# First expert pair: token rows gathered straight into turned form, shorter norm and mask steps, another order of the last output quarters

## The reference, cut to what matters

```python
x = x + jnp.einsum('bte,ed->btd', merged, w_out)
h2 = rmsnorm(x, ffn_norm_w)                       # mean of squares, + EPS, rsqrt, times the weight
x = x + moe_ffn(h2, w_router, b_router, w_up, b_up, w_down, b_down)

def moe_ffn(h, ...):                              # 264 tokens, 32 experts, D = 1024
    logits = h @ w_router + b_router
    top_vals, top_idx = lax.top_k(logits, 4)      # ties go to the lower expert
    gates = softmax(top_vals)
    ...                                           # for each expert e, on the rows of its tokens:
    u = xb @ w_up[e] + b_up[e]                    # 1024 -> 2048
    a = glu * sigmoid(1.702 * glu) * (lin + 1)    # glu, lin: even and odd columns, clamped at 7
    y = a @ w_down[e] + b_down[e]                 # 1024 -> 1024, times the gate, added to its token
```

## Time and profile before

| | |
|---|---|
| median of three runs | 1151.85 us |
| the profiled execution's own time | 1151.45 us |
| its span (first to last instruction) | 1149.5 us |
| busy: TensorE, VectorE, ScalarE | 95%, 39%, 16% |
| TensorE's granted clock | 0.993 of full speed |
| moved by the transfers | 444.34 MB, 387 GB/s over the span |
| share of the chain that ended last | TensorE 61%, DMA 36% |

### The profile page before, as it was taken

How to read it: one execution, slowest core, us unless ns; L and a number is a source line. 1 busy time by engine, 2 the same in 40 slices (tenths; PEclk the granted TensorE clock), 3 DMA queues, 4 the chain that set the end, 5 groups by cost and what they waited for, 6 DMA issues and landing times.

```text
span 1149.5 us, 14796 instructions
## 1 busy us (share of the span) xinstructions
PE 1095.8 (95%) x5914; PEld 495.3 (43%) x5943; DVE 444.3 (39%) x878; ACT 184.8 (16%) x394; POOL 88.5 (8%) x161
## 2 busy tenths in 40 slices
PE   9999999999999999999999999999999999999997
PEld 6688898553333333333333333333333333333332
DVE  4867786753343233232323232323232323232322
ACT  2133231220321111010101010101010101010101
POOL 1775115000000000000000000000000000000000
PEclk9999999999999999999999999999999999999999
DMA  9945639989999999999999999999999999999996
GB/s 318 328 135 158 196 92 341 399 328 429 422 418 427 424 429 433 432 429 433 433 429 433 433 429 433 434 428 434 433 428 434 433 428 434 433 428 434 425 423 267
DMA packets 52628, 444.34 MB, mean 387 GB/s; under 512 B 13037, under 2 KB 19309, under 8 KB 35677
## 3 DMA queue, kind: packets, MB, share of 16 engines
q1 hardware_dynamic: 46136, 435.83, 91.0%
q0 software_dynamic: 5600, 7.32, 2.4%
q10 hardware_dynamic: 852, 0.64, 0.2%
HBM read 439.78 MB, written 2.37 MB: 385 GB/s over the span
## 4 chain that ended last, share of the span: by engine, by line
PE 61%; DMA 36%; DVE 1%; ACT 1%; issue 1%; SPq 0%; ACTq 0%
PE pA L1964 30%; PE pB L1964 23%; DMA ring<-in_w_up 21%; DMA ring<-in_w_down 10%; PE pM L1964 6%; DMA area<-in_w_up 5%; PE pM L1967 1%; PE pA L1967 1%; ACT area L1199 0%; DVE x L1816 0%; DVE hn L1858 0%; DVE area L1860 0%; DVE area L1852 0%; ACT area L1176 0%; ACT area L1028 0%
## 5 line engine op out<-in xcount | busy, mean ns | idle before, releaser
L1964 PE MATMUL pA<-ring,hn 128*64 128x512 f32 x1536 | 354.2, 604 | 23.0 <-DMA ring<-in_w_up 23.0
L1964 PEld LDWEIGHTS pA<-ring,hn 128*64 128x64 f32 x1536 | 105.4, 138 | 220.3 <-issue 187.4
L1964 PE MATMUL pB<-ring,area 128*64 128x512 f32 (+2 forms) x784 | 171.5, 591 | 6.6 <-DMA ring<-in_w_down 5.7
L1964 PE MATMUL pB<-area,ring 128*128 128x132 f32 (+2 forms) x928 | 140.3, 342 | 0.5 <-ACT area L1028 0.5
L1964 PE MATMUL pA<-area,hn 128*64 128x512 f32 x512 | 119.3, 610 | 9.9 <-DMA area<-in_w_up 9.8
L1964 PEld LDWEIGHTS pB<-area,ring 128*128 128x128 f32 (+1 forms) x928 | 115.7, 175 | 22.4 <-issue 3.2
L1964 PEld LDWEIGHTS pB<-ring,area 128*64 128x64 f32 (+2 forms) x784 | 58.5, 136 | 101.1 <-issue 87.8
L1816 DVE TENSOR_TENSOR x<-pM,x 128x512 f32<-128x512 f32 x60 | 40.1, 691 | 148.2 <-PE pM L1964 148.1
L1187 ACT ACTIVATE area<-area 128x512 f32<-128x512 f32 x30 | 18.9, 631 | 386.3 <-DVE area L1799 386.3
L1731 DVE COPY conv_row<-pM 128x512 f32<-128x512 f32 x30 | 20.6, 686 | 146.2 <-PE pM L1964 146.2
L1964 PE MATMUL pB<-area 128*64 128x512 f32 (+2 forms) x300 | 67.2, 550 | 1.2 <-DVE area L1264 1.2
(11 more groups left out here) (335 smaller groups left out, 936.6 us busy)
## 6 DMA issues: line engine op xcount, KB each, us to landing
ring<-in_w_up SPq DMA_DIRECT2D x36, 4096.0 KB, 29.8
ring<-in_w_down SPq DMA_DIRECT2D x18, 4096.0 KB, 29.2
area<-in_w_up SPq DMA_DIRECT2D x12, 4096.0 KB, 30.2
ring<-in_w_up SPq DMA_DIRECT2D x17, 2048.0 KB, 15.2
area<-in_w_down SPq DMA_DIRECT2D x6, 4096.0 KB, 30.0
ring<-in_w_in SPq DMA_DIRECT2D x22, 1024.0 KB, 12.1
ring<-in_w_up SPq DMA_DIRECT2D x14, 1024.0 KB, 8.9
ring<-in_w_down SPq DMA_DIRECT2D x13, 1024.0 KB, 25.9
```

The source lines that it names most:

```text
L1964: return pe.matmul(out, w, m, start=start, stop=stop, skip_group_check=True)
```

## The change

Four things are changed.

1. The gather of the first pair works the other way round: eight groups of 128 columns of `hn` (every fourth column of a half, so that the order is that of the weights' rows) are stationary, `pick` moves, and the product stands in PSUM in turned form at once. The copies to `xrow` and the eight transposes are gone; VectorE multiplies each pair of groups from PSUM into `xsT`. Groups 0 to 3 stand before `up(0)`, the three products of each of groups 4 to 7 stand between `up(1)` and `up(2)`.
2. `rms`: the scale by 1/D and the addition of EPS are done by ScalarE's root.
3. The mask: the count of larger logits is the start of the running sum, in place of an operation of its own.
4. `BRANCH`: both pieces of the last half product stand together, `x_cols` 4 and 5 behind them, `ahead` is gone, and the first transpose of `x_cols` 4 releases the place of chunk 5.

```diff
-          ("logits", 0), ("part", (0, 6, KT)), ("half", 0), ("part", (1, 0, 4)), ("count", 0), ("part", (1, 4, 6)),
-          ("x_cols", 4), ("part", (1, 6, KT)), ("half", 1), ("ahead", 1), ("x_cols", 5), ("rms", 1), ("logits", 1),
-          ("gather", 1), ("count", 1), ("gather", 2)]
+          ("logits", 0), ("part", (0, 6, KT)), ("half", 0), ("part", (1, 0, 4)), ("count", 0), ("part", (1, 4, KT)),
+          ("half", 1), ("x_cols", 4), ("x_cols", 5), ("rms", 1), ("logits", 1),
+          ("gather", 1), ("count", 1)]
...
-            return pB[:, n, 0:256] if n < 2 else pA[:, 512 * n:512 * n + 256]
+            if n == 0:
+                return pB[:, :, 0:128]
+            if n == 1:
+                return pA[:, 1024:2048].rearrange("p (k c) -> p k c", k=2)[:, :, 0:128]
+            return pA[:, 512 * n:512 * n + 256].rearrange("p (k c) -> p k c", k=2)
...
-                    nc.scalar.activation(stat[0:r, 8 + a:9 + a], stat[0:r, 8 + a:9 + a], ACT.Sqrt).then_inc(norm_rt, 1)
+                    s1 = stat[:, 5:6] if a == 1 else stat[0:r, 2 * a + 1:2 * a + 2]
+                    nc.scalar.activation(stat[0:r, 8 + a:9 + a], s1, ACT.Sqrt, bias=stat[0:r, 62:63],
+                                         scale=1.0 / D).then_inc(norm_rt, 1)
...
-            for n in (1, 3):
-                act.wait_ge(first_full, n + 1)
-                f = slice(256 * n, 256 * n + 256)
-                nc.scalar.activation(xrow[:, f], first_xs(n), ACT.Copy).then_inc(first_rows_act, 1)
...
-                    V.tensor_scalar(stat[0:r, 8 + a:9 + a], s1, 1.0 / D, EPS, ALU.mult, ALU.add).then_inc(norm_in, 1)
...
-                    V.tensor_scalar(stat[rows_, 56 + a:57 + a], stat[rows_, 56 + a:57 + a], -1.0, float(TOPK),
-                                    ALU.mult, ALU.add)
-                    link(V.tensor_tensor_scan(rank[rows_, :], cst[rows_, C_ONE:C_ONE + NE], e, 0.0,
+                    link(V.tensor_tensor_scan(rank[rows_, :], cst[rows_, C_ONE:C_ONE + NE], e, stat[rows_, 56 + a:57 + a],
...
-            for n in (0, 2):
+            for n in range(4):
                 dve.wait_ge(first_full, n + 1)
-                f = slice(256 * n, 256 * n + 256)
-                V.tensor_copy(xrow[:, f], first_xs(n)).then_inc(first_rows, 1)
                 if n == 0:
                     dve.wait_ge(fnorm_loaded, 16)
-                for k in (n, n + 1):
-                    V.tensor_tensor(xsT[:, 2 * k:2 * k + 2, :], misc_bank()[:, 0:256].rearrange("p (k s) -> p k s", k=2),
-                                    fw[:, 2 * k:2 * k + 2, :], ALU.mult).then_inc(misc_free, 1)
+                V.tensor_tensor(xsT[:, 2 * n:2 * n + 2, :], first_xs(n),
+                                fw[:, 2 * n:2 * n + 2, :], ALU.mult).then_inc(first_rows, 1)
...
-            def first_gather(n):
-                return matmul(first_out(n), pick[:, 0].rearrange("p e s -> p (e s)"), piece(hn[:, 0, :], n), stop=False)
+            def turned(t, k):
+
+                h = 512 * (k // ROWS)
+                return t[:, h + k % ROWS:h + 512:ROWS]
+
+            def first_gather(k):
+
+                matmul(first_xs(k // 2)[:, k % 2], turned(hn[:, 0, :], k), pick[:, 0].rearrange("p e s -> p (e s)"), stop=False)
+
+            def first_samples(k):
+
+                matmul(first_xs(k // 2)[:, k % 2], turned(s_parts[0:96], k), s_pick[0:96].rearrange("p e s -> p (e s)"),
+                       start=False, stop=False)
+
+            def first_rest(k):
+
+                mm = matmul(first_xs(k // 2)[:, k % 2], turned(hn[:, 1, :], k), pick[:, 1].rearrange("p e s -> p (e s)"),
+                            start=False)
+                if k % 2:
+                    mm.then_inc(first_full, 1)
...
-                    if a == 2:
+                    if a in (2, 4):
                         mm.then_inc(ring_free, 1)
...
-                    for k in range(2 if a == 1 else 0, KT):
+                    for k in range(KT):
...
-            for n in range(4):
-                matmul(first_out(n), pick[:, 1].rearrange("p e s -> p (e s)"), piece(hn[:, 1, :], n),
-                       start=False).then_inc(first_full, 1)
-                if n:
-                    if n < 3:
-                        first_turn(n - 1)
+            for k in range(ROWS):
+                first_rest(k)
...
                     if first and e == 0:
-                        if c == 1:
-                            first_turn(2)
-                            first_turn(3)
-                        pe.wait_ge(misc_free, FILL["x_turn", c])
+                        if c == 2:
+                            for k in range(ROWS, KT):
+                                first_gather(k)
+                                first_samples(k)
+                                first_rest(k)
+                        pe.wait_ge(first_rows, c + 1)
```

More of the change, by code:

```diff
@@ L265 @@
 FILL, _n = {}, 0
-for _s in STEPS + BRANCH + [("x_turn", n) for n in range(4)]:
+for _s in STEPS + BRANCH:
     _n += FILLS_OF.get(_s[0], 1)
@@ L1605, in _ @@
             V.tensor_copy(count_w.rearrange("p a n -> p (a n)"), cst[:, C_TRI:C_TRI + 256])
+            V.memset(stat[:, 62:63], EPS)
             dve.wait_ge(wr_loaded, 32)
@@ L2210, in half_part @@
                 return mm
-            def piece(t, n):
-                f = t[:, 512 * (n // 2):512 * (n // 2) + 512].rearrange("p (i r) -> p i r", r=ROWS)
-                return f[:, :, 2 * (n % 2):2 * (n % 2) + 2]
-            def first_out(n):
-                return first_xs(n).rearrange("p (i r) -> p i r", r=2)
-            def first_gather(n):
-                return matmul(first_out(n), pick[:, 0].rearrange("p e s -> p (e s)"), piece(hn[:, 0, :], n), stop=False)
+            def turned(t, k):
[11 more added lines that the diff above has]
+                    mm.then_inc(first_full, 1)
             for what, a in BRANCH:
@@ L2259, in _ @@
                     mm = columns(a, x, b)
-                    if a == 2:
+                    if a in (2, 4):
                         mm.then_inc(ring_free, 1)
-                elif what == "ahead":
-                    b = pM[:, (fills.n + 1) % 2, :]
-                    pe.wait_ge(misc_free, fills.n)
-                    for k in range(2):
-                        mm = matmul(b[:, 0:NE], hT[:, k, 128:256], w_router_sb[:, k, :], start=(k == 0), stop=False)
-                        if k == 0:
-                            mm.then_inc(ring_free, 1)
                 elif what == "logits":
@@ L2290, in _ @@
                         pe.wait_ge(hn_ready, 2)
-                        for n in range(3):
-                            first_gather(n)
-                        continue
-                    first_gather(3)
-                    pe.wait_ge(s_parts_ready, 1)
-                    pe.wait_ge(s_pick_ready, 1)
-                    for n in range(4):
-                        matmul(first_out(n), s_pick[0:96].rearrange("p e s -> p (e s)"),
-                               piece(s_parts[0:96], n), start=False, stop=False)
+                        pe.wait_ge(s_parts_ready, 1)
+                        pe.wait_ge(s_pick_ready, 1)
+                        for k in range(ROWS):
+                            first_gather(k)
+                            first_samples(k)
                 elif what == "count":
@@ L2321, in _ @@
             pe.wait_ge(hn_ready, 3)
-            def first_turn(n):
-                b = misc_bank()
-                if n % 2:
-                    pe.wait_ge(first_rows_act, n // 2 + 1)
-                else:
-                    pe.wait_ge(first_rows, n // 2 + 1)
-                for k in range(2):
-                    mm = tr(b[:, 128 * k:128 * k + 128], xrow[:, 256 * n + k:256 * n + 256:2])
-                mm.then_inc(misc_full, 1)
-            for n in range(4):
-                matmul(first_out(n), pick[:, 1].rearrange("p e s -> p (e s)"), piece(hn[:, 1, :], n),
-                       start=False).then_inc(first_full, 1)
-                if n:
-                    if n < 3:
-                        first_turn(n - 1)
+            for k in range(ROWS):
+                first_rest(k)
             def gather(b, half, freed=False, parts=True):
```

9 lines of the change are left out of this document (5 added, 4 removed).

## The result

The changed kernel takes 1155.85 us (median of 6 runs, 1154.18 to 1158.46), the one before took 1151.68 us in 6 runs (1150.22 to 1152.98): a ratio of 1.0042 with an interval of 1.0032 to 1.0052. The prediction was 1151.6 us, within 0.2%, with a range that ended at 1153.4; it was wrong. TensorE reaches the third up product of the first expert 4 us later than before, and most of that lateness is carried to the end of the kernel.

What follows compares the result with a forecast made beforehand. It took the weight stream to bound the kernel from 260 us; an earlier chunk 5 and a later `up(2)` netted -0.2 us, so the profiled 1151.45 became 1151.25, plus 0.4 for the median: 1151.6 us, range 1149.6 to 1153.4.

Steps and rivals of the forecast that it cites:

- The turned product's price: Gather on TensorE: each float32 turned product with strided loads takes 0.34 us, so the block of twelve lasts 3.1 us.
- above 0.36: Price per turned product beyond which the delay exceeds 1.6 us and the kernel turns slower.
- my bounds, 0.21 and 0.55: Price range of a turned float32 product: low if strided loads cost nothing extra, high if load and streaming never overlap.
- The slack of 1.6 us: Weight stream at 318.6 us: the tightest piece, 5.8 us to landing against 4.2 needed, can absorb 1.6 us of lateness.
- the forecast's own 1.4 late: TensorE starts `up(2)` at 252.25 us, 1.4 us later than before, because of the block of twelve products.
- the thin stretch: Weight stream at 252 us, 217 GB/s, where 1.9 us were lost; forecast to move to 256 to 258 us.
- the piece at 318: Transfer of 0.5 MB issued at 318.6 us, the tightest later place, with 1.4 of its 1.6 us slack used.
- bound by the stream behind 260 us: From 260 us the weight transfers, at 424 to 431 GB/s, set the end, which moves only if the whole stream shifts.
- instead of 1.1: `up(0)` starts at 241.4 us, 1.1 us earlier, as copy, transposes and their hand-overs are gone.
- Rival B: Strided loads not hidden: block 5.0 us, `up(2)` 4.7 late, time 1155.0; chance 0.08 for +0.5 to +2.3, 0.07 beyond.
- Chunk 5: Weight chunk released by the first transpose behind the half products: issued at about 234.2 us, 0.25 us earlier.
- VectorE's longer stand: VectorE stays at `first_full` 3 and 4 until 252.6 us; covered, with 1.5 us of its 4.7 us wait left.

Runs made afterwards that it cites:

- e13: Kernel before plus a test stretch of products whose stationary operand takes every 1st to 5th column, ahead of `up(2)`; its total time is of no use, only load records count.
- e2: Changed kernel with the turned products' stationary operand read from neighbouring columns (wrong columns gathered, same sizes): 1151.6 us, ratio 1.0003.
- e5: Changed kernel with hn written by ScalarE in the order in which it is read, so all loads are contiguous and columns right: 1153.0 us, ratio 1.0011.
- e1: Kernel before with only the new quarter order (`x_cols` 4 behind the half product, no `ahead`): 1151.8 us, ratio 1.0003.
- e3: Kernel before plus two unread products of 128x512 float32 from constants ahead of `up(2)`, a pure delay: 1152.84 us, ratio 1.0019.
- e4: Kernel before plus four unread products of 128x512 float32 from constants ahead of `up(2)`, a pure delay: 1154.79 us, ratio 1.0032.
- e7: Kernel before with only the norm's and mask's shorter steps: 1150.51 us, ratio 0.9996.
- e12: Kernel before with new order and shorter steps, hn written in turned order, old gather and transposes now with contiguous operands: 1150.91 us, ratio 0.9993.
- e14: Kernel before without the four products of k = 5 in the first expert's `up(2)`, making TensorE earlier: 1150.05 us, ratio 0.9992.
- e15: The same kernel as e12 run again, against the kernel before: 1151.09 us, ratio 0.9995.
- e6: Changed kernel with products of 192 and 320 columns put into TensorE's waits for the logits and the pick: 1156.25 us, ratio 1.004.
- e11: Kernel before with new order and steps, groups 0 to 3 gathered and transposed as before, 4 to 7 by strided turned products: 1156.15 us, ratio 1.0036.
- e8: The changed kernel run again, unedited, against the kernel before: 1155.69 us, ratio 1.0037.
- e10: Changed kernel with the old quarter order and `ahead` put back: 1155.13 us, ratio 1.0032.

## Why the prediction was wrong, by its own steps

**The turned product's price, the step that failed first.** I took 0.34 us, from the spacing of transposes whose loads also take every fourth column, and said that the mechanism turns slower above 0.36. It was mis-sized: 0.235 a load in e13, 0.49 a product in the block (4.36 less four bfloat16 products at some 0.1, over 8). The block cost 4.36 and not 3.1. The earlier trace rows had misled me: I read there 212 ns for the strided load and expected about 260 for hn, but the transposes' records in a stretch of mixed operations say little about loads back to back. It lay between my bounds, 0.21 and 0.55, and much nearer the upper. In the traces of e2 and e5 contiguous loads shorten the block by 1.94 and 1.93 us. Against the two runs of the changed kernel (1.0042, 1.0037) they give 1.0003 and 1.0011, so 3.0 to 4.5 us less; what is over 1.9 us of that isn't explained by the block.

**The clock, which was not in the sum at all.** In the traces of the changed kernel it stood at 1.2 GHz into `up(0)`, which cost 0.66 us in one and 1.8 in the other. The last four products ahead of `up(0)` took 2.17 us where I had forecast 1.36 and the tail, but 4 x 0.49 = 1.96 of that is their price, and only some 0.2 the clock. It fell in all eight traces with a changed gather, and in none of nine without (before, e1, e3, e4, e7, e12, e13, e14, e15). What in the gather does it is not settled: not the two waits (e6), not the strided loads (e2, e5), not the short products ahead of `up(0)` alone (e11). Nor are short products enough, wherever they stand: e13 ran thirty of them behind `up(1)`, six at each distance, at 1.00. Before held 1.00 with TensorE at 0.46 in one us:

```profile
238.00:239.00 1.00, 0.46 (x4) 0.43 (x5) 0.53 (x4) 0.99 (x2) 0.00 (x0) 1.00 0.95 410
```

**The slack of 1.6 us, the step that gave the sign.** With the measured block and clock, the forecast's own chain would still have said 4.0 late less 1.6 of slack, so 2.4 us, and with the forecast's own 1.4 late it said nothing is lost. e3 and e4 refute the slack: 1.91 us of delay costs 2.2, 3.63 costs 3.7. I compared one piece's time to landing (5.8 us) with what an empty queue needs (4.2) and took the difference for room. The windows from the anchor show what became of it. In the first 30 us the transfers lose less than TensorE's lateness: 0.4 us in e3 (late 2.0), 2.2 in e4 (3.7), 2.4 in after (4.0), 3.8 in e8 (5.2). That is the thin stretch, which takes up some 1.5 us, as the forecast had it. In the next 90 us, around the piece at 318, they lose the rest: 1.5, 1.8, 2.2 and 1.6 us, so that the sum is about the whole lateness each time (1.9, 4.0, 4.5 and 5.4 before rounding of the parts). The 1.6 us that I counted as slack there are about what is paid there.

The transfers run at 420 GB/s and not 431 in this place already before, at a DMA share of 1.00 or 1.01, and with a delay at 411 in e3, 406 in e4 and 401 in after. The landing time of a piece shrinks meanwhile, which looked like slack being used. I had judged the stream by rows of 400 to 800 us and by one piece, and never by a window around it; 300 to 350 us was there to be read, at 420. And I had called the kernel bound by the stream behind 260 us, though TensorE waits for no transfer until 500: up to there the slots are released by a TensorE that is simply later. Why the rate is lower there was not tried.

**Put together**, for the profiled execution, from the anchor: `up(0)` 0.28 early instead of 1.1; `up(0)` itself +0.66; the transposes gone, -0.68; the block +4.36: 4.05 late, the rest of the span 3.4. Had the price been 0.34 and the clock held, by one to one the 1.4 of my sum would have made 1151.85 + 1.4, about 1153.2, just inside the range. Rival B was right in kind, "the strided loads are not hidden", and near in size, 4.7 late, 1155.0, but partly by luck: its price of 0.55 was too high, it had no clock, and it took off the slack of 1.6. I gave it 0.15 in all, and 0.07 to what was measured, because I priced at the transposes' spacing; a price that I knew only between 0.21 and 0.55, with a turning point at 0.36, did not bear so small a chance.

**What held.** Chunk 5 left 0.29 us earlier, counted from the anchor, where I had worked out 0.25. The norm and mask steps gave nothing that can be told (e7), nor did the order (e1, e10). VectorE's longer stand was covered: its last turned product began at 254.34 behind a wait of 1.66, and afterwards it still waited for `up(3)`:

```profile
254.34 0.42 DVE L1739 TENSOR_TENSOR hn<-pA,fnorm 128x256 f32<-128x256 f32 x1 [1.66 <-PE pA L1959]
```

```profile
DVE conv_row L1794 <- PE pA L1959: 1.4, 1, 1.4
```

That wait was 4.7 before; I had 1.5. That this fits is luck in part: VectorE was through 6.8 us later and not 4.6, the product 3.4 later and not 1.4, and the two errors cancel. The thin stretch moved from 252 us to between 256 and 260, where I had 256 to 258, and it is emptier, 25 GB/s in its worst us where before had 217:

```profile
257.00:258.00 1.00, 1.00 (x8) 0.29 (x4) 0.93 (x6) 0.00 (x0) 0.00 (x0) 1.00 0.06 25
```

**The size of the change.** The copy and the transposes that it removed had lain in TensorE's waits for pick and copy; the block that replaced them lies where TensorE has none. With contiguous loads that is some 2 us (e5 against e12 and e15), with the distance of four 3.0 to 4.5 more. Part of both may be the clock, whose share the timed runs don't separate.

## What to carry to other kernels

Before trading transposes for products with a turned stationary operand, look at where each lies (work in a wait cost nothing here, a block between two full products did) and at how its load reads memory: keep it at neighbouring or every-second float32, or write the tile once in the order in which it will be read. To judge whether a delay reaches a stream of transfers, take the rate in a window around its tightest place, not one piece's time to landing: if it is under the loop's rate, count on no slack. And see whether the engine that releases the slots ever waits for a transfer: where it doesn't, its delay moves every release behind it.

## What the runs showed of the hardware that was not expected

- A float32 load of 128 columns takes 192, 196, 261, 329 and 321 ns at distances of 1 to 5 elements (e13), a bfloat16 one 222 at 4 against 100 (after, e5); two loads go with each float32 product.
- ScalarE's copy of 1024 float32 columns took 2.14 us when it read four elements apart, 1.15 when contiguous (e5).
- The granted clock was at 1.2 GHz for 3.4 to 6.9 us in all eight traces with the changed gather, with the engine fully busy from 237 to 243 us in one of them (e6), and at no time from 225 to 262 us in the nine others.
- At a DMA share of 1.00 or 1.01 the transfers moved 414 to 420 GB/s from 300 to 350 us where TensorE was not late (before, e1, e7, e12, e14, e15) and 401 to 411 where it was some 2 us late or more (after, e2 to e6, e8 to e11); among the latter the rate doesn't follow the lateness.
